# Seven products instead of eight for the last eight row tiles of an output projection

## The reference, cut to what matters

```
def hybrid_layer(h, pos, topk, pre_w, post_w, w_in, ...):
    ...
    mix = jnp.concatenate([pool_out, ssd_out, attn_out], axis=-1)
    out = jnp.einsum('bte,ed->btd', mix, w_out)
    return h + rmsnorm_2(out, post_w)
```

## Time and profile before

| | |
|---|---|
| median of 3 runs | 3311.01 us (3302.79 to 3314.41) |
| profiled execution: span | 3303.0 us; no other time of that execution is recorded |
| PE busy | 3261.9 us, 99% of the span |
| DVE busy | 1770.4 us, 54% |
| ACT busy | 727.7 us, 22% |
| mean granted clock of TensorE | 0.996 of full speed |

### The profile page before, as it was taken

One profiled execution on the slowest core, in us unless ns is written; L12 is line 12 of the kernel. 1 busy time (PEld: TensorE's weight loads), 2 busy tenths in 40 slices (PEclk: granted clock), 3 DMA queues, 4 the chain that ended last, 5 costly groups with the idle time before them and its releaser, 6 DMA issues.

```text
span 3303.0 us, 60784 instructions
## 1 busy us (share of the span) xinstructions
PE 3261.9 (99%) x25782; PEld 2995.1 (91%) x25782; DVE 1770.4 (54%) x3270; ACT 727.7 (22%) x1971; POOL 45.2 (1%) x83
## 2 busy tenths in 40 slices
PE   9999999999999999999999999999999999999999
PEld 7998889988999998888999997899879999988898
DVE  2545565414768651613455656666345566566652
ACT  1212211111011201011111225422131122253221
POOL 1000000000000000000000000000000000000000
PEclk9999999999999999999999999999999999999999
DMA  6453344453444303554444544333344545524432
GB/s 222 146 179 117 97 128 153 154 178 109 140 142 140 103 4 129 194 159 115 149 158 147 160 150 132 128 108 123 121 137 152 179 143 165 167 89 128 152 105 102
DMA packets 436203, 454.65 MB, mean 138 GB/s; under 512 B 25051, under 2 KB 412576, under 8 KB 435648
## 3 DMA queue, kind: packets, MB, share of 16 engines
q1 hardware_dynamic: 433344, 443.69, 42.3%
q0 software_dynamic: 2128, 5.19, 0.5%
q10 hardware_dynamic: 464, 1.90, 0.2%
HBM read 448.67 MB, written 2.10 MB: 136 GB/s over the span
## 4 chain that ended last, share of the span: by engine, by line
PE 96%; DVE 2%; ACT 1%; DVEq 1%; issue 0%; ACTq 0%; POOL 0%; POOLq 0%
PE bank L377 39%; PE bank L524 10%; PE bank L2247 9%; PE bank L315 5%; PE bank L558 5%; PE bank L2465 3%; PE bank L1872 3%; PE bank L1360 3%; PE bank L2357 1%; PE bank L2372 1%; PE bank L2393 1%; PE bank L2388 1%; PE bank L2382 1%; PE bank L2364 1%; PE bank L2376 1%; PE bank L2331 1%
## 5 line engine op out<-in xcount | busy, mean ns | idle before, releaser
L377 PE MATMUL bank<-xnT,ring 128*128 128x128 f32 (+1 forms) x4800 | 593.0, 280 | 2.2 <-ACT wk L1020 1.0
L377 PEld LDWEIGHTS bank<-xnT,ring 128*128 128x128 f32 x4800 | 575.9, 191 | 5.7 <-issue 4.4
L524 PE MATMUL bank<-xnT,ring 128*128 128x256 f32 x1536 | 343.0, 382 | 0.4 <-ACT G L430 0.4
L377 PE MATMUL bank<-hT,ring 128*128 128x128 f32 (+1 forms) x2816 | 339.0, 279 | 0.6 <-ACT G L405 0.5
L377 PEld LDWEIGHTS bank<-hT,ring 128*128 128x128 f32 x2816 | 330.2, 191 | 1.4 <-ACT G L405 1.4
L524 PEld LDWEIGHTS bank<-xnT,ring 128*128 128x128 f32 x1536 | 289.8, 191 | 40.3 <-ACT G L430 0.6
L2247 PE MATMUL bank<-xnT,ring 128*128 128x272 f32 (+1 forms) x1344 | 310.9, 390 | 0.0
L2247 PEld LDWEIGHTS bank<-xnT,ring 128*128 128x128 f32 x1344 | 252.6, 190 | 44.5
L442 DVE TENSOR_TENSOR ring<-ring 128x1024 f32<-128x1024 f32 x100 | 122.5, 1225 | 237.1 <-PE bank L377 194.0
L377 PE MATMUL bank<-G,ring 128*128 128x128 f32 (+1 forms) x1792 | 225.4, 279 | 0.0
L377 PEld LDWEIGHTS bank<-G,ring 128*128 128x128 f32 x1792 | 215.5, 191 | 0.0
(11 more groups left out here) (607 smaller groups left out, 4172.5 us busy)
## 6 DMA issues: line engine op xcount, KB each, us to landing
ring<-in_w_in SPq DMA_DIRECT2D x155, 2048.0 KB, 8.3
ring<-in_w_out SPq DMA_DIRECT2D x16, 3072.0 KB, 11.0
ring<-in_w_out SPq DMA_DIRECT2D x16, 2048.0 KB, 9.3
ring<-in_w_br SPq DMA_DIRECT2D x12, 2048.0 KB, 8.4
ring<-in_w_in SPq DMA_DIRECT2D x6, 512.0 KB, 8.0
G<-in_x POOLq DMA_DIRECT2D x2, 1024.0 KB, 8.9
wk<-in_pool_w POOLq DMA_DIRECT2D x2, 1024.0 KB, 9.2
out<-G SPq DMA_DIRECT2D x8, 256.0 KB, 2.3
```

Of the source, the lines that this page charges most:

```text
L377: mm = pe.matmul(out_, weights[:, k, :], x(k), start=(start and k == 0), stop=(k == HALF - 1), skip_group_check=True)
L524: mm = pe.matmul(bank[j][:, META:T], ring[:, s, k, j * P:(j + 1) * P], xnT[:, k, META:T], start=(k == 0), stop=(k == KT - 1))
```

## The change

The tail becomes eight units of the same seven-product form, one for each pair of output tiles (`unit_pe` with `short=tail`). A quarter now has four row tiles, so a product is 8 records. The kernel's bookkeeping of units gets a record (`Unit`) with each unit's weight quarters, sums, corner bank and temporary row.

New work on DVE: the four weight sums of each unit, on 128x512 elements (those of unit 0 are put into head 7 of attention, ahead of that head's last multiply); four combined inputs (`tail_turned`) after attention, on which product 3 of unit 0 waits; the adds that finish a unit; one add of a pair of tiles to `xnT` (`tail_merge`), in place of two adds from PSUM. ACT gets five copies a unit, and does the squares of unit u-1 within unit u, between its third and its fourth copy. The running sum of squares now ends with tile 13, and PE adds the squares of tiles 14 and 15 with the matrix of ones.

```
+    def short_quarters(s, part):
+        w = wide[:, s]
+        low, high, c = w[:, 0:W8 // 2], w[:, W8 // 2:W8], BLK * part
+        return low[:, :, c:c + P], high[:, :, c:c + P], low[:, :, c + P:c + 2 * P], high[:, :, c + P:c + 2 * P]
...
     def unit_pe(...):
...
+            half = W8 // 2 if short else HALF
...
             product(wbank(work["pe"].n)[:, lo:MID], a12, lambda k: b2[:, k, lo:MID], True).then_inc(work_full, 1)
+            if turned:
+                pe.wait_ge(S["st_turned"], turned)
...
     layers_pe
-                for s in range(SLOTS):
-                    loaded(s)
-                    for j in range(4):
-                        pe.wait_ge(proj_free, tiles["pe"].go())
-                        for k in range(W8):
-                            mm = pe.matmul(bank[j % 2][:, m0:T], wide[:, s, k, j * P:(j + 1) * P], mix[SUB + k][:, m0:T],
-                                           start=(k == 0), stop=(k == W8 - 1))
-                        mm.then_inc(proj_full, 1)
-                    if s == 2 and layer != LAST:
+                for u in range(OUTS):
+                    unit_pe(pe, u // 2, m0, *tail_turned, short=tail, part=u % 2,
+                            turned=None if u else count["pe"]["st_turned"].go())
+                    if u == 5 and layer != LAST:
...
                 wait("rms_sq", KT)
+                pe.matmul(b[:, m0:T], ones, squares[:, KT - 2, m0:T], start=False, stop=False)
                 pe.matmul(b[:, m0:T], ones, squares[:, KT - 1, m0:T], start=False, stop=True).then_inc(work_full, 1)
...
     layers_act
-                for k in range(KT):
+                def tail_squares(u):
                     wait("b2_in")
-                    act.activation(squares[:, k, m0:T], xnT[:, k, m0:T], ACT.Square, scale=SQ).then_inc(S["rms_sq"], 1)
+                    for k in (2 * u, 2 * u + 1):
+                        act.activation(squares[:, k, m0:T], xnT[:, k, m0:T], ACT.Square, scale=SQ).then_inc(S["rms_sq"], 1)
+                for u in range(OUTS):
+                    d1, d2 = (tail_parts[u % 2][:, j, :] for j in range(2))
+                    if u >= 2:
+                        act.wait_ge(S["tail_used"], OUTS * layer + u - 1)
+                    unit_first_act(act, d1, m0)
+                    unit_second_act(act, d1)
+                    unit_third_act(act)
+                    if u:
+                        tail_squares(u - 1)
+                    unit_fourth_act(act, d2)
+                    unit_last_act(act, d2, m0)
...
+                tail_squares(OUTS - 1)
                 rms_root_act(act, m0)
     layers_dve, head 7
+                    if h == 7:
+                        v.wait_ge(S["so_full"], 6 * (OUTS * layer + OUTS - 1) + 4)
+                        unit_sums12_dve(v, units["dve"].now())
+                        unit_sums34_dve(v, units["dve"].now())
                     v.tensor_tensor(attn[:, h, m0:T], full()[:, m0:T], a_gate[:, h, m0:T], ALU.mult).then_inc(work_free, 1)
                 to("b2_pe")
+                x12_, x22_, x21_, x11_ = tail_turned
+                low, high = tail.first, tail.second
+                v.tensor_tensor(x12_, low[:, :, MID:T], low[:, :, META:MID], ALU.subtract)
+                v.tensor_tensor(x21_[:, :, META:MID], high[:, :, MID:T], low[:, :, MID:T], ALU.subtract)
+                if m0 == 0:
+                    v.tensor_scalar(x21_[:, :, 0:META], low[:, :, 0:META], -1.0, None, ALU.mult)
+                    v.tensor_copy(x11_[:, :, 0:META], high[:, :, 0:META])
+                v.drain()
+                v.tensor_tensor(x22_, high[:, :, MID:T], x12_, ALU.subtract)
+                v.drain()
+                v.tensor_tensor(x11_[:, :, META:MID], high[:, :, META:MID], x22_, ALU.subtract)
+                to("st_turned")
                 out_ends(OUTS - 1)
...
+                def tail_merge(u):
+                    v.drain()
+                    v.wait_ge(proj_free, tiles["dve"].now() + 2)
+                    pair = xnT[:, 2 * u:2 * u + 2, m0:T]
+                    v.tensor_tensor(pair, pair, tail_parts[u % 2][:, :, m0:T], ALU.add).then_inc(S["tail_used"], 1)
                     to("b2_in")
+                def tail_sums(u):
+                    for k in (2 * u, 2 * u + 1):
                         wait("rms_sq")
...
                             v.tensor_tensor(own, own, sq, ALU.add)
                         v.drain()
...
+                for u in range(OUTS):
+                    d1, d2 = (tail_parts[u % 2][:, j, :] for j in range(2))
+                    unit_first_dve(v, d1, m0)
+                    if u + 1 < OUTS:
+                        unit_sums12_dve(v, n0 + u + 1)
+                    if u:
+                        tail_merge(u - 1)
+                    if u + 1 < OUTS:
+                        unit_sums34_dve(v, n0 + u + 1)
+                    if u > 1:
+                        tail_sums(u - 2)
+                    unit_ends_dve(v, d1, d2)
+                    tiles["dve"].go()
+                tail_sums(OUTS - 2)
                 v.nop().then_inc(S["rms_acc"], 1)
+                tail_merge(OUTS - 1)
```

More of the change, by code:

```diff
@@ L9 @@
+from collections import namedtuple
 from contextlib import ExitStack
@@ L138 @@
 N_P2 = len(STACKS2) + 3
+Unit = namedtuple("Unit", "slot used quarters sums corner row")
+Short = namedtuple("Short", "sums rows x0 first second")
 class Turn:
@@ L369, in unit_pe @@
             own = bank[(t - 1) % 2]
[L370 to L373, removed]
+            u = uses["pe"][s].go(0 if part else 1)
+            half = W8 // 2 if short else HALF
+            parts, unit_sums = (short_quarters(s, part), short.sums) if short else (quarters(s), sums)
+            rows = short.rows if short else t5_at
+            x0 = short.x0 if short else 0
+            b1, b2 = (short.first, short.second) if short else (xnT[:, 0:HALF], xnT[:, HALF:KT])
+            a11, a12, a21_less, a22 = parts
+            s1, s2, s4 = unit_sums
             def product(out_, weights, x, start):
-                for k in range(HALF):
-                    mm = pe.matmul(out_, weights[:, k, :], x(k), start=(start and k == 0), stop=(k == HALF - 1),
+                for k in range(half):
+                    mm = pe.matmul(out_, weights[:, k, :], x(k), start=(start and k == 0), stop=(k == half - 1),
                                    skip_group_check=True)
@@ L389, in unit_pe @@
             pe.wait_ge(work_free, work["pe"].go())
-            unit_banks.append(wbank(work["pe"].n))
-            corner = unit_banks[n][:, MID:T]
+            corner_bank = wbank(work["pe"].n)
+            made_units.append(Unit(s, u, parts, unit_sums, corner_bank, rows[n % 2]))
+            corner = corner_bank[:, MID:T]
             product(corner, s1, lambda k: x12[:, k, :], True).then_inc(S["st_full"], 1)
@@ L418, in unit_third_act @@
                 act.wait_ge(S["st_dve"], n - 1)
-            act.activation(t5_at[n % 2], corner, ACT.Copy).then_inc(S["st_act"], 1)
+            act.activation(made_units[n].row, corner, ACT.Copy).then_inc(S["st_act"], 1)
         def unit_fourth_act(act, d2):
@@ L434, in unit_sums12_dve @@
         def unit_sums12_dve(v, n):
[L436 to L439, removed]
+            unit = made_units[n]
+            a11, a12, a21, a22 = unit.quarters
+            s1, s2, s4 = unit.sums
+            v.wait_ge(w_loaded[unit.slot], 16 * unit.used)
             if n:
@@ L446, in unit_sums34_dve @@
         def unit_sums34_dve(v, n):
-            s, u = unit_slots[n]
-            a11, a12, a21, a22 = quarters(s)
-            s1, s2, s4 = sums
+            a11, a12, a21, a22 = made_units[n].quarters
+            s1, s2, s4 = made_units[n].sums
             v.tensor_tensor(a21, a11, a21, ALU.subtract).then_inc(S["st_sum"], 1)
@@ L2116, in build @@
         out_banks = []
+        tail_turned = [flat(g[0])[:, a:a + n * W8 // 2].rearrange("p (k t) -> p k t", t=n)
+                       for a, n in ((0, P), (512, P), (1024, MID), (1600, MID))]
+        tail_space, tail_rest = flat(merged[:, 0:8]), flat(rest)
+        tail = Short([tail_space[:, 512 * i:512 * (i + 1)].rearrange("p (k c) -> p k c", c=P) for i in range(3)],
+                     [tail_rest[:, 1088 + P * i:1088 + P * (i + 1)] for i in range(2)], 0,
+                     g[1][:, 0:W8 // 2], g[1][:, W8 // 2:W8])
+        tail_parts = [rest[:, 2 * i:2 * i + 2] for i in range(2)]
         def begin(layer):
@@ L2188, in layers_load @@
                 last_use[3] = (S["so_dve"], OUTS * (layer + 1))
+                units["sp"].go(OUTS)
                 for s in range(SLOTS):
@@ L3157, in layers_dve @@
                 to("heads_done")
[L3158 to L3161, removed]
+                def tail_merge(u):
[3 more added lines that the diff above has]
+                    v.tensor_tensor(pair, pair, tail_parts[u % 2][:, :, m0:T], ALU.add).then_inc(S["tail_used"], 1)
                     to("b2_in")
-                    if k:
+                def tail_sums(u):
```

(10 more changed lines are left out.)

30 lines of the change are left out of this document (15 added, 15 removed).

## The result

The changed kernel took **3323.39 us** (median of 5 runs, 3320.42 to 3327.67), the kernel before, beside it, 3311.01 us (5 runs, 3302.37 to 3314.41): a ratio of 1.005 [1.0034, 1.0066], slower by about half a per cent. The two profiled executions have spans of 3321.1 and 3303.0 us, 18.1 apart, at the same mean granted clock of 0.996.

The account below looks back on a forecast made before the run. PE's rate of products alone was taken to bound the old tails. -11.1 (shorter products) + 22.5 (pauses) + 2.7 (start) + 2.4 (end) = +16.5 us on the median 3311.0 gave 3327.5 us, range 3317 to 3339.

Parts of the forecast that it names:

- the first case: Both tails: product 7 waits for ACT's fourth copy in units 1 to 6; 3327.5 us in total, chance 0.80.
- Saving on PE: Both tails: seven shorter products a unit save 5.2 us in layer 1 and 5.9 in layer 0, together -11.1 us.
- Pauses before product 7: Units 1 to 6: PE waits for the fourth copy, 1.89 us in layer 1, 1.86 in layer 0, +22.5 us.
- Before the first unit: Tail start: unit 0's sums cost nothing; product 3 waits for combined inputs, +1.3 us layer 1, +1.4 layer 0, together +2.7.
- The end: After the last product: late merge, squares and table load delay the logarithm by 1.2 us a layer, +2.4 us.
- Weights: Tail weight loads: the second is there near 3234, its first reader comes near 3239; no cost, 5 us to spare.
- layer 0's: Layer 0's tail, start to logarithm: shorter products, waits for copies and inputs, and later logarithm, 7.9 us more.
- Rival 2: Tails: the granted clock falls after each of twelve pauses, 23 us more, 3350 us; chance 0.05.
- The prediction's own sign against it: Both tails: the forecast is wrong if their granted clock is under 1.
- The rule weighed in the prediction: PE in the tails: brief, frequent idling can swing the clock between two levels; total +39 rather than +16 us.
- Rivals 1 and 3: Tails: 1, fourth copy isn't held, 3305 us, chance 0.11; 3, strided DVE operations at twice their price, 3344, chance 0.04.
- The product with ones for tile 14: After the last unit: two added PE records, 0.43 us, lie under the table load; without that cover 0.4.

Follow-up runs that it names:

- the kernel with the merge first: Changed kernel with tail_merge(u-1) moved on DVE ahead of the next unit's first two weight sums: 3302.74 us, 0.9984 of the kernel before.
- the run with the old sum: Changed kernel with tile 14's square added to the running sum by DVE again, PE adding only tile 15's: one run, 3326.53 us.
- the run with the merge last: Changed kernel with tail_merge(u-1) moved behind all four weight sums of the next unit: 3354.09 us, 1.0142 of the kernel before.
- the shorter end: Merge ahead of the sums, combined inputs made early, last pair merged and squared tile by tile, against the changed kernel: 3299.12 us, 0.9969 of before.

## Why the prediction came out

The forecast was the first case, the pauses, at 3327.5 us in 3317 to 3339, and it held: 3323.4, +18.1 us by the profiles where +16.5 was worked out. Term by term:

- **Saving on PE.** Without pauses a unit takes 6.25 us in layer 1 and 6.60 in layer 0 (period of the kernel with the merge first), just as the record prices of the earlier trace rows gave.
- **Pauses before product 7.** 8.12 - 6.25 = 1.87 us in layer 1 (forecast 1.89). In layer 0 the starts of 2378.34 and 2386.78 below give 8.44 - 6.60 = 1.84 (1.86). Six a layer, in units 1 to 6. The merge, which no row gave, took 0.69 and 0.72. The two runs that undo one link each on DVE and on ACT show the chain: either takes all twelve pauses away. That the size fits to 0.02 us is partly luck. In layer 1 PE resumes 3.38 us after the end of product 4 (forecast 3.51), mostly because it starts 0.05 us behind the copy where the earlier trace rows gave 0.14; and the 24 records behind a pause take 0.11 us more than without one, which the sum had only in its bounds.
- **Before the first unit.** Product 3 starts 3.16 us after product 1 in layer 0 (2354.64 to 2357.80) and 3.29 in layer 1 (3237.53 to 3240.82): +1.2 and +1.5, together the 2.7 forecast, but it was worked out as +1.4 and +1.3, so the match is luck. In layer 1 DVE is idle for 0.43 us ahead of its third combination, where 0.08 is usual, and the trace names no wait for it. In the run with the old sum, which leaves these operations and their inputs as they are, the gap is not there, and PE waits 0.90 us for these inputs instead of 1.24. The sums in head 7 cost nothing: PE's wait at the start of each tail is as long as before.
- **The end.** 3.44 us from product 7 to logarithm in both layers: +1.0 and +1.1, forecast 1.2 each.
- **Weights.** No wait, as forecast.

**The term that was mis-sized** is layer 0's: 7.9 forecast, 9.4 measured. One pause of its six was longer, and the clock fell behind it:

```profile
2378.34 3.21 PE L392 MATMUL bank<-G,ring 128*128 128x144 f32 x24 [1.58 <-ACT merged L442]
...
2386.78 3.21 PE L392 MATMUL bank<-G,ring 128*128 128x144 f32 x24 [1.58 <-ACT merged L442]
...
2395.57 4.83 PE L392 MATMUL bank<-G,ring 128*128 128x144 f32 x24 [1.93 <-ACT merged L442]
```

```profile
2386.78:2395.57 8.79, 6.86 (x56) 6.67 (x56) 5.08 (x11) 2.05 (x7) 0.00 (x0) 1.00 0.74 236
2395.57:2400.20 4.63, 4.63 (x24) 4.63 (x25) 1.85 (x5) 0.58 (x2) 0.00 (x0) 0.65 0.02 7
```

DVE's first sum of that unit came 0.35 us later than in the others, PE stood idle for 1.93 us by the timeline instead of 1.58, and the next 24 records ran at a granted clock of 0.65: 4.63 us instead of 3.04. That is 0.35 + 1.6 = 2.0 us, more than the difference; the layer's other terms came out some 0.5 us under the forecast. Rival 2 was dismissed on a stretch at full clock whose 2.2 us without PE are three idle times, the longest of 1.72 us. It came true for one pause of twelve, at a price of 1.6 us where it had 1.9; in the run with pauses of 3 us it came true for eight. The prediction's own sign against it, a granted clock under 1 in the tails, is met in layer 0, with 0.97. The rule weighed in the prediction (the Trainium skill, TensorE: Matmul & The Clock Gate, "A second HAM failure mode: psum-queue depth-cycling") is borne out here in part: eleven idle times of about 1.6 us kept 1.00, the one of 1.93 did not.

The late sum is at the same unit in the repeat of the changed kernel, with the same fall behind it:

```profile
2396.47:2401.10 4.63, 4.63 (x25) 4.63 (x26) 1.85 (x5) 0.58 (x2) 0.00 (x0) 0.66 0.01 2
```

In the runs with the merge last and with the old sum, too, the fifth unit's first sum comes after 1.91 us of idle time where most of the others have 1.55. In the run with the old sum PE's pause there is 1.94 us, and the clock is 0.65 behind it. The late sum is thus tied to a place of the program. What holds DVE there is not shown; it stays open.

**Rivals 1 and 3** fell by the trace: product 7 is held twelve times, and a sum of 512 elements takes 0.69 us, not twice that. Rival 1's case, a fourth copy that isn't held, is what the two reorderings bring about. The kernel with the merge first then came out at 0.9984 of before, the small gain that rival 1 named (3305 of 3311).

**One reading was wrong without harm.** The product with ones for tile 14 was counted as hidden, 0.4 us without cover. It is hidden, but it also spares PE the wait for DVE's last add, which in the run with the old sum is 2.41 us, with a low clock behind it, and costs 0.9 to 1.2 us a layer. The end would have cost some 2 us a layer without it.

The median stands 4 us under the forecast although the profiles lie further apart than forecast. The sum was put on the median of three runs, 3311.0; in the runs beside the repeat the kernel before had 3308.0. At an equal mean clock of 0.996 the runs have medians of 3305.01 (before, 16 runs) and 3322.99 us (changed, 4 runs), 18.0 apart. So the difference was forecast 1.5 us too small, and the median's miss to the other side comes from the base.

## What to carry to other kernels

When an instruction stream per engine is in order, price a change by the queue ahead of the instruction that the bottleneck waits for: here two weight sums stood ahead of an add, the add ahead of a square, and the square ahead of a copy that PE needed, 1.9 us in each of twelve units, though neither add nor square was urgent. Before giving up on cheaper arithmetic, move such work behind or well ahead of the urgent copy: one swapped line turned +0.5% into -0.16%. And a short pause on PE can cost twice: by its length and, where the granted clock falls behind it, by the slower records that follow.

## What the runs showed that was not expected

- The granted clock can fall after short pauses within dense work. In the tails of the changed kernel, its repeat and the run with the old sum it never fell after the eleven idle times of about 1.6 us, and each time behind the one of 1.93 or 1.94 us (0.65, 0.66 and 0.65 over the next 24 records). It fell after eight of twelve pauses of about 3 us, and to 0.54 after 2.41 us at the end of layer 1 with the old sum. It stayed at 1.00 after the 3.31 us of the run with the merge last and the 2.02 us at the end of layer 1 with the shorter end. What decides is not shown.
- The runs' spread follows the clock. In the 56 runs of the kernel before beside the experiments, the median was 3302.4 us at a mean granted clock of 0.997, 3305.0 at 0.996, 3307.7 at 0.995, 3310.2 at 0.994 and 3314.4 at 0.993: some 3 us for each thousandth.
- A request for a table that is already loaded loads it again, for the full 1.28 us.
